# Hybrid decoder step: index keys fetched in 2 KB pieces, the sample's pieces spread over the gathers, tile 0's value rows shared out by stage

## What is computed

```
z = x @ w_in                        # heads of both mixers, token indexer, gates
y_a = sparse attention: index score I[t,s] = sum_h w[t,h] relu(q_idx[t,h].k_idx[s]),
      the best 128 (prompt) or 256 (sample) keys per query, softmax over them
y_b = forgetting attention: softmax(q.k/8 + sum of log f between key and query)
h = LN1(a*x + w_out(sig(g_a)*(y_a@w_branch_a) + sig(g_b)*(y_b@w_branch_b)))
x = LN2(a*h + PEER(h))
PEER: 8 heads pick 16 of 16384 experts each; per token sum over 128 experts of
      gate * gelu(u_e . h) * v_e,   u_e and v_e rows of 1024 floats
```

## Time and profile before

| | us |
|---|---|
| median of 3 runs | 2494.94 |
| lowest, highest | 2492.96, 2496.37 |
| the profiled execution, its own time | 2496.61 |
| span of its trace | 2494.8 |
| busy: PE, DVE, GpSimd, ACT | 1870.8, 1664.1, 1344.5, 433.0 |
| DMA moved | 791.69 MB, of it 604.58 MB by GpSimd's queue |

### The profile page before, as it was taken

How to read it: one execution, slowest core, us unless ns; L and a number is a source line. 1 busy time by engine, 2 the same in 40 slices (tenths; PEclk the granted TensorE clock), 3 DMA queues, 4 the chain that set the end, 5 groups by cost and what they waited for, 6 DMA issues and landing times. The chain is left out here.

```text
span 2494.8 us, 23480 instructions
## 1 busy us (share of the span) xinstructions
PE 1870.8 (75%) x6566; PEld 909.3 (36%) x6566; DVE 1664.1 (67%) x3371; ACT 433.0 (17%) x1052; POOL 1344.5 (54%) x1174
## 2 busy tenths in 40 slices
PE   8999998979759736326767677667678986667686
PEld 6756644735335412102222223233234542222231
DVE  2114886798784997987997575489555469745544
ACT  0123533101011201101111022122121121111110
POOL 1100000357755656655445467756767668877775
PEclk9998987989979868659887899889889998899999
DMA  4205330889989989999999999989999999899997
GB/s 182 63 12 168 96 119 9 314 319 386 409 293 340 317 253 385 402 396 348 377 381 350 367 381 380 390 326 358 400 405 409 409 397 344 332 372 410 408 394 294
DMA packets 258180, 791.69 MB, mean 317 GB/s; under 512 B 30562, under 2 KB 55203, under 8 KB 257347
## 3 DMA queue, kind: packets, MB, share of 16 engines
q0 software_dynamic: 166400, 604.58, 63.4%
q1 hardware_dynamic: 90692, 180.59, 20.6%
q10 hardware_dynamic: 960, 5.03, 0.5%
HBM read 783.90 MB, written 5.59 MB: 316 GB/s over the span
## 5 line engine op out<-in xcount | busy, mean ns | idle before, releaser
L1214 PE MATMUL ps<-arena 128*128 128x512 f32 (+1 forms) x1600 | 845.4, 664 | 310.5 <-DMA arena<-peer_v,arena 263.5
L820 POOL DMA_INDIRECT arena<-peer_u,arena x576 | 671.9, 1167 | 610.5 <-DVE arena L1823 317.7
L1860 DVE CUSTOM_DVE_ANT_0 arena<-arena 128x1024 f32<-128x1024 f32 x576 | 694.0, 1226 | 394.3 <-DMA arena<-peer_u,arena 385.7
L820 POOL DMA_INDIRECT arena<-peer_v,arena x576 | 653.2, 1134 | 390.0 <-PE ps L1214 178.0
L1214 PEld LDWEIGHTS ps<-arena 128*128 128x128 f32 (+1 forms) x1600 | 300.0, 203 | 798.6 <-issue 628.0
L1869 DVE SCALAR_TENSOR_TENSOR arena<-arena 128x1024 f32<-128x1024 f32 x171 | 219.9, 1286 | 128.9 <-DMA arena<-peer_v,arena 124.1
L1512 ACT ACTIVATE arena<-arena 128x128 f32<-128x128 f32 (+1 forms) x400 | 149.4, 394 | 728.5 <-PE ps L1214 725.1
L1037 PE MATMUL ps<-arena 128*128 128x448 f32 (+2 forms) x512 | 158.0, 468 | 22.6 <-DVE arena L1763 21.9
L1069 PE MATMUL ps<-arena 128*128 128x128 f32 (+2 forms) x768 | 149.4, 354 | 3.0 <-ACT arena L1400 3.0
L849 PE MATMUL ps<-arena 128*128 128x296 f32 (+1 forms) x512 | 130.7, 415 | 10.5 <-DMA arena<-w_proj 10.5
L1190 PE MATMUL ps<-arena 128*64 128x512 f32 (+1 forms) x512 | 90.7, 501 | 61.3 <-DMA arena<-v_b 61.3
(11 more groups left out here) (192 smaller groups left out, 1648.7 us busy)
## 6 DMA issues: line engine op xcount, KB each, us to landing
arena<-k_b SPq DMA_DIRECT2D x128, 256.0 KB, 20.8
arena<-v_b SPq DMA_DIRECT2D x128, 256.0 KB, 15.4
arena<-w_mix SPq DMA_DIRECT2D x56, 512.0 KB, 6.7
arena<-w_q SPq DMA_DIRECT2D x48, 512.0 KB, 6.6
arena<-kv_a SPq DMA_DIRECT2D x128, 128.0 KB, 15.1
arena<-w_out SPq DMA_DIRECT2D x24, 512.0 KB, 6.7
arena<-peer_u,arena POOLq DMA_INDIRECT x576, 9.1
arena<-peer_v,arena POOLq DMA_INDIRECT x576, 6.8
```

The source lines that it names most:

```text
L820: pool.indirect_dma_start(out=rows[slot_of[n]], out_offset=None, in_=io["peer_v"] if v else io["peer_u"], in_offset=bass.IndirectOffsetOnA ...
L1214: last = pe.matmul(bank(6 + a, 512, 0, nt), diag_p[read_before[n] % ND][:, 0:nt], rows[slot_of[n]][:, a * 512:(a + 1) * 512], start=(k == ...
L1860: dve.tensor_tensor_reduce(out=row, in0=row, in1=h, scale=1.0, scalar=0.0, op0=ALU.mult, op1=ALU.add, accum_out=pre[:, k:k + 1]).then_inc( ...
```

## The change

Four things are edited.

1. **Index keys** come as 16 rows of 2 KB a page: partition 16b + p holds features 4p to 4p + 3 of sequence b. A chunk is then eight products over 64 partitions each (four features groups r, for two halves g of the partitions), in place of four over 128.
2. **Index queries and new keys** go through a DRAM tensor: five stores from `heads` after the first four weights in `prompt()`, and, after `x_rows(0)` and a wait for the stores, sixteen loads into `qis` and `kin`, ahead of the fifth weight. DVE's 18 copies go.
3. **Plan of the sample**: chunk 1 comes 22 gathers after chunk 0's sums rather than 48, the forgetting pieces 7 apart rather than 5, the wait ahead of `s_out` 8 gathers rather than 16. By the list's own sums: chunk 1 at gather 216 (242 before), chunks 2 and 3 at 219 and 224, the new keys at 229, the first forgetting piece at 237 (263), the top-8 rounds from 238 to 554 (264 to 502), `s_max` of pairs 1, 2, 3 at 351, 431, 511 (347, 407, 467), of pairs 4 to 7 at 573, 618, 663, 708 (529, 582, 635, 688), the end at 738 (726), SWITCH at 762 (750), merge 2 until 818 (806).
4. **Tile 0's v rows**: three of four on DVE for k below 16 (as before), all on DVE for k from 16 to 63, every other one from 64 on. DVE takes 92 (96 before), PE 36 (32).

```diff
+        qsc = nc.dram_tensor("index_of_sample", [64, NB, NI + 1, SN], F32, kind="Internal").ap()
@@ read_by_dve
             if i == 0:
-                return k % 4 != 3
+                return k % 4 != 3 if k < 16 else k < 64 or k % 2 == 0
@@ sample_items
-            out = [(("zero",), 0), (("spread", 0), 1), (("ix", 0), 3), (("iy", 0), 48), (("ix", 1), 3)]
+            out = [(("zero",), 0), (("spread", 0), 1), (("ix", 0), 3), (("iy", 0), 22), (("ix", 1), 3)]
-            out += [(("s_score", 0, c), 5) for c in range(5)]
+            out += [(("s_score", 0, c), 7) for c in range(5)]
-                g = 5 if q < 4 else 3
+                g = 7 if q < 4 else 3
-                        out += [(("s_score", q + 1, c), 5), (("s_weigh", q, c), 5)]
+                        out += [(("s_score", q + 1, c), 7), (("s_weigh", q, c), 7)]
-                    out += [(("s_out", q), 16)]
+                    out += [(("s_out", q), 8)]
@@ sync, prompt()
                 for w in range(NMW):
                     weights(w)
+                for h in range(NI + 1):
+                    sp.dma_start(qsc[:, :, h, :], heads[0:64, QI + h, LP:T].rearrange("p (b t) -> p b t", t=SN)
+                                 ).then_inc(qsc_stored, 16)
...
                 x_rows(0)
+                sp.wait_ge(qsc_stored, 16 * (NI + 1))
+                for b in range(NB):
+                    c0 = b % 4 * 32
+                    of_b = qsc.rearrange("(p r) b h t -> b p r h t", r=4)[b]
+                    sp.dma_start(qis[16 * b:16 * b + 16, :, c0:c0 + 32], of_b[:, :, 0:NI, :].rearrange("p r h t -> p r (h t)")
+                                 ).then_inc(qsc_loaded, 16)
+                    sp.dma_start(kin[16 * b:16 * b + 16, :, :], of_b[:, :, NI, :]).then_inc(qsc_loaded, 16)
...
+                sp.wait_ge(qsc_loaded, 16 * 2 * NB)
@@ sync, sample()
-                            sp.dma_start(ring[s_][p0:p0 + 64, at + j % 4 * 128:at + (j % 4 + 1) * 128],
-                                         io["kidx"].rearrange("(n d) k -> n d k", d=64)[bass.ds(no, 1)].rearrange(
-                                             "o d k -> (o d) k")).then_inc(ring_loaded[s_], 16)
+                            sp.dma_start(ring[s_][16 * b:16 * b + 16, j % 4 * 512:(j % 4 + 1) * 512],
+                                         io["kidx"].rearrange("(n p r) k -> n p (r k)", p=16, r=4)[bass.ds(no, 1)].rearrange(
+                                             "o p x -> (o p) x")).then_inc(ring_loaded[s_], 16)
@@ tensor, index_products
-                keys = unit("ki", -1, c, 0).rearrange("p (a n) -> p a n", a=4) if c < 4 else kin
-                for g in range(2):
-                    for p in (2 * g, 2 * g + 1):
-                        last = pe.matmul(bank(2 * (c % 2) + g, w), qis[:, p, :], keys[:, p, :], start=(p % 2 == 0),
-                                         stop=(p % 2 == 1))
-                    last.then_inc(ix_ready, 1)
+                keys = unit("ki", -1, c, 0).rearrange("p (j r k) -> p r j k", j=4, r=4) if c < 4 else kin
+                for r_ in range(4):
+                    for g in range(2):
+                        p0 = 64 * g
+                        last = pe.matmul(bank(2 * (c % 2) + g, w), qis[p0:p0 + 64, r_, :], keys[p0:p0 + 64, r_],
+                                         start=(r_ == 0), stop=(r_ == 3))
+                        if r_ == 3:
+                            last.then_inc(ix_ready, 1)
@@ vector, project()
-                dve.wait_ge(zero_set, 1)
-                for h in range(NI):
...
-                last.then_inc(spread_d, 1)
```

More of the change, by code:

```diff
@@ L337, in program @@
         o_ready, o_copied = sem("o_ready"), sem("o_copied")
-        spread_a, spread_d = sem("spread_a"), sem("spread_d")
+        spread_a = sem("spread_a")
         wrow_spread, wd_ready = sem("wrow_spread"), sem("wd_ready")
@@ L342, in program @@
         b0_ready, b0_mixed, ln0_loaded = sem("b0_ready"), sem("b0_mixed"), sem("ln0_loaded")
+        qsc_stored, qsc_loaded = sem("qsc_stored"), sem("qsc_loaded")
         ix_ready, ix_read, iy_ready, iy_read = (sem(n) for n in ("ix_ready", "ix_read", "iy_ready", "iy_read"))
@@ L726, in sample @@
                         nos = page_numbers(b * NPG + 4 * c0, 4 * (c1 - c0))
-                        p0, at = 64 * (b % 2), b // 2 * 512
                         for j, no in enumerate(nos):
                             s_ = c0 + j // 4
-                            sp.dma_start(ring[s_][p0:p0 + 64, at + j % 4 * 128:at + (j % 4 + 1) * 128],
-                                         io["kidx"].rearrange("(n d) k -> n d k", d=64)[bass.ds(no, 1)].rearrange(
-                                             "o d k -> (o d) k")).then_inc(ring_loaded[s_], 16)
+                            sp.dma_start(ring[s_][16 * b:16 * b + 16, j % 4 * 512:(j % 4 + 1) * 512],
+                                         io["kidx"].rearrange("(n p r) k -> n p (r k)", p=16, r=4)[bass.ds(no, 1)].rearrange(
+                                             "o p x -> (o p) x")).then_inc(ring_loaded[s_], 16)
                 for z, (kind, q, c, e) in enumerate(fill_list):
@@ L1601, in project @@
                     dve.tensor_copy(kan[64 * g:64 * g + 64, :], heads[0:64, KA + g, LP:T])
-                dve.wait_ge(zero_set, 1)
-                for h in range(NI):
-                    for e in range(2):
-                        for pp in range(2):
-                            c0 = (2 * pp + e) * 32 + h * 8
-                            dst = qis.rearrange("p (a b) c -> p a b c", b=2)[64 * e:64 * e + 64, :, pp, c0:c0 + 8]
-                            src = heads[0:64, QI + h, LP:T].rearrange(
-                                "p (a b e t) -> p a b e t", b=2, e=2, t=SN)[:, :, pp, e, :]
-                            dve.tensor_copy(dst, src)
-                for e in range(2):
-                    last = dve.tensor_copy(
-                        kin[64 * e:64 * e + 64, :, :],
-                        heads[0:64, KI, LP:T].rearrange("p (a e t) -> p a e t", e=2, t=SN)[:, :, e, :])
-                last.then_inc(spread_d, 1)
             norms = [0]
```

## The result

The changed kernel takes 2538.03 us (median of 4 runs, 2531.97 to 2538.5) beside 2495.65 us for the kernel before in the same runs: a ratio of **1.0169** (95% interval 1.0141 to 1.0197). The forecast was 2489.6 us, 0.2% faster, with a range up to 2514. The profiled execution has a span of 2536.1 us against 2494.8, 41.3 us more.

A forecast was written before the change was run, and what follows sets the result against it. The prediction took the kernel for a DMA-bound gather stream that loses time where the DMA share is below 1.03. Terms 1 - 1 + 7.7 - 13 = -5.3 us gave a median of 2489.6 us; range 2470 to 2514.

The forecast's parts named there:

- The prompt, +1: Prompt: stores and loads ahead of the fifth weight delay PE, costing 1 us (0 to 6).
- Merge 1 and the keys, -1 and +7.7: Merge 1 to first forgetting piece: better-travelling key pieces give -1 us; PE's wait at chunk 1 costs net +7.7 us.
- don't hold the start of the 96: SP's queue: chunk 0's 32 DMAs follow merge 1's last weight, which moves up, so the 96 key DMAs aren't delayed.
- the 969 that was to decide for rival (a): First forgetting piece: forecast at 958.5 us; a start later than 969 us would decide for late keys.
- rival (a): Chunk 1 to first forgetting piece: SP stays at 0.469 us, halves don't overlap; +23 us, 2512.6 us; chance 0.27.
- The spacing, -13: Sample: forgetting pieces 7 apart, rounds spread and s_max of pair 2 behind tile 2's routing; -13 us (-23 to 0).
- the four dips that it named: Sample, at 1120, 1170 to 1200, 1300 to 1330 and 1410 us: DMA share falls, losing 4.1, 6.0, 6.6 and 4.6 us.
- The sign that waits for k_b and v_b fall to less than half of 134 us: Forgetting pairs: PE's waits for pages of k and v should drop below half of 134 us.
- Rival (b): Sample: the spacing recovers nothing; only the two blocked stretches gain, 5 us rather than 13; 2497.6 us; chance 0.12.
- rival (c): More dips go: the 1170 us chain is eased too, SP's DMA takes its low end; 12 us less, 2477.6; chance 0.18.
- The sparse stage, 0: Sparse pairs: 8 gathers less for pages costs 0, since 4 MB have 18 gathers (23 us) until wanted.
- Merge 2 later, 0: Merge 2: ends at 818, still ahead of tile 4's routing at 830, so costs 0.

The follow-up runs named there:

- experiment 1: Changed kernel with the index queries' stores and loads moved behind the prompt's ten weight transfers; 1.0087 of before, then 1.0114 beside the changed kernel's 1.0183.
- experiment 3: Kernel before with only tile 0's new v-row rule: 0.9979 of before; with only the new key layout, its bounce behind the prompt's weights: 0.9981; with both: 0.9966.
- experiment 6: Changed kernel with forgetting pieces 5 apart, later pieces held in place: 1.012 of before, against 1.0183; kernel before with s_out 8 and pieces 6 apart: 1.007.
- experiment 8: Kernel before with the sample's end 12 gathers later (738): 1.0027 of before; kernel with new v rows and key layout, end at 716: 0.995.

## Why the prediction was wrong

**The prompt, +1.** Wrong by 11.5 us, in size. The kinds of cost were right, stores and loads ahead of the fifth weight. The forecast had the loads at 0.33 to 0.57 us from the earlier trace rows, in all 5 to 9 us; most took 0.59 each and the first two 4.9 together, in all 14.2. It had the stores at 3 to 5 us; they took 6.4. Then 0 to 5 us of wait at PE became a +1, while PE waited 10.7 us, and as far as experiment 1 can tell nothing behind it gives that back. "Their 32-byte pieces have no like in the trace" called for a wide bound, and it had 0 to 6.

**Merge 1 and the keys, -1 and +7.7.** Right in the main. The key scores' gain (17.4 of 19), SP's DMA (0.316 us, forecast 0.332), chunk 1 at 920.9 us where the prompt isn't late (918), PE's wait (28 to 53; 30.3), GpSimd stopping at 227 gathers (226), 244 issued at the first forgetting piece (245). The stretch cost 10.0 us for 6.7; the -1 in it, for pieces that travel better, no run tells apart. One sentence was wrong: that chunk 0's DMAs "don't hold the start of the 96". The last weight moves up far less than the merge (issued until 797.8 us in experiment 3, 799.4 before), and chunk 0 then keeps SP until 838.5 us, past the key scores' end at 834.9. With DMAs of 0.316 us that costs some 3 us; with 0.469 it took back nearly the whole gain (experiment 3). The first forgetting piece started at 972.0 us, later than the 969 that was to decide for rival (a). It was late by the prompt's 12.5 us, not by rival (a)'s causes: SP at 0.469 us or halves that don't overlap, and neither was so. The sign didn't tell a late start from slow keys. The Trainium skill ("TensorEngine Tiling (Array Packing)", Tiling Modes) lists 64x128 as two tiles and says that tiles can work in parallel. The trace agrees: 3.72 us for eight products over half the partitions, 3.6 for four over all.

**The spacing, -13.** In size right, -14.1; in cause in part. Three of the four dips that it named are gone, some 10 us less with the new small ones counted in; the rest of the 14.1 no window shows, and a kernel with the old spacing gained 10.3 us in this stretch when it came late into it (experiment 6). The sign that waits for k_b and v_b fall to less than half of 134 us failed: they fell to 92.5. Rival (b), a gain of 5 us, doesn't fit the stretch; rival (c) falls, since the dip that it wanted eased grew from 6.0 to 8.1 us.

**The sparse stage, 0.** This is the step that failed: "pages of 4 MB have 18 gathers (23 us) until they are wanted", costed at 0. The stretch measured +25.3 us, and s_out 8 by itself made the kernel before 20 us slower. The forecast set 23 us against 4 MB, which at 408 GB/s would take 10, but pages share the engines with the gathers, and their pieces are a quarter as long: 60 us from first issue to the last fill in use. The symptom was named (waits of the sparse scores for kv_a), the price was not, and the trace of before had it: 34.4 us of SP to issue a pair's 32 DMAs, and 52 us from the first of them to the product that needs the last fill, which PE still waited 2.5 us for. By the Trainium skill ("DMA: Bandwidth & Descriptors", Queues, rings and completion order) a DMA engine takes turns between its queues packet by packet. That a queue of short pieces gets the smaller share by this is our reading; the page doesn't say it. Landing times of 14.8 us for 128 KB in pieces of 1 KB and 11.8 for 256 KB in pieces of 2 KB fit it, as does the result of reading 2 KB; the taking of turns itself no run shows.

**Merge 2 later, 0.** Wrong: 0.27%, 7 us, by experiment 8 (2 to 11 us by its interval), and +7.6 in the trace. "Still ahead of tile 4's routing" looked at one neighbour; where merge 2 meets the switch of the buffers was not looked at.

So the mechanism behind the forecast's sign was no single rival. Its rival for slower had the place wrong, the keys; 37 of the 46.6 us missed are the prompt's "+1" and the sparse pages' "0".

## What to carry to other kernels

A step that a change makes tighter is not costed at zero because its bytes fit: take how long such a transfer takes in the trace beside the traffic it will meet, and compare that with the time left. Stores and loads of a new detour belong behind the transfers that the next product waits for. A dip that is gone from a window of the clock may have moved with the program: look for it at its own place. And of a change with several parts, the parts may have opposite signs: here two gave 0.3% together, and the rest took 2%.

## What the runs showed of the hardware

Three things had not been expected. Pages in pieces of 1 KB beside gathers of 4 KB pieces arrived so late that reading 2 KB instead, with half the DMAs, took away the whole 1.2 to 1.8% that the changed kernel had lost, and 0.33% of the kernel before. DMAs of 64 rows, of 2 KB as of 512 bytes, took SP 0.469 us, against 0.333 for 128 rows and 0.316 for 16; into 64 partitions the engines moved 303 to 317 GB/s at a share of 1.04. By the Trainium skill ("DMA: Bandwidth & Descriptors", The descriptor swizzle) each engine of a transfer to 128 partitions writes one port, those for partitions 0 to 63 the even ones and the others the odd ones. The page has this for transfers that GpSimd issues, and no run here shows the ports; since the DMAs in question alternate between the two halves of the partitions, it doesn't explain the loss by itself. And the kernel before took 2496 or 2536 to 2548 us, by the set of runs and so by the chip or the hour, with 363 instead of 408 GB/s in a window of its last stretch.
